# One row-maximum instruction and one eviction instruction for both heads of a softmax step

## The reference, cut to what matters

```python
# forgetting attention, 8 heads of 64, blocks of 128 queries, causal
logits = einsum('bhqd,bhkd->bhqk', qh, kh) + F_t - F_s        # masked above the diagonal
p = softmax(logits, axis=-1);  out = einsum('bhqk,bhkd->bhqd', p, v)
# cross attention, 4 heads of 256, 256 keys, no mask
p = softmax(q @ k.T / sqrt(256));  o = p @ v
# GQA, 8 query heads of 64 over 2 key heads, 512 keys, no mask
p = softmax(q @ k.T / 8);  o = p @ v
```

## Time and profile before

| | |
|---|---|
| median of 3 runs | 1402.72 us (1400.03 to 1402.81) |
| the profiled execution | 1399.9 us, its span 1398.1 us |
| granted TensorE clock, mean over the span | 0.994 |
| busy: PE, PEld, DVE, ACT, POOL | 1361.8, 1095.2, 660.2, 619.4, 613.9 us |
| `fox`: first scores to first product of the memory norm | 207.6 to 253.5 us |
| `xat`: first scores to the last product's start | 402.0 to 438.8 us |
| `gqa`: first scores to the first product of `out2` | 916.9 to 979.3 us |

### The profile page before, as it was taken

How to read it: one execution, slowest core, us unless ns; L and a number is a source line. 1 busy time by engine, 2 the same in 40 slices (tenths; PEclk the granted TensorE clock), 3 DMA queues, 4 the chain that set the end, 5 groups by cost and what they waited for, 6 DMA issues and landing times.

```text
span 1398.1 us, 17303 instructions
## 1 busy us (share of the span) xinstructions
PE 1361.8 (97%) x6544; PEld 1095.2 (78%) x6544; DVE 660.2 (47%) x973; ACT 619.4 (44%) x861; POOL 613.9 (44%) x448
## 2 busy tenths in 40 slices
PE   9999999999989999999999999988999999999999
PEld 7877955788876888888888887854878888888887
DVE  5434938355433444344343316588255555554111
ACT  5555228553444443434442123587245545554111
POOL 3444320374430456555564543411325555556453
PEclk9999999999999999999999999999999999999999
DMA  7222212142220244344436433200312222323422
GB/s 267 91 90 94 87 41 81 61 173 99 91 90 1 91 144 141 135 159 141 150 135 260 177 135 105 91 31 30 121 61 90 90 90 92 118 90 135 175 96 90
DMA packets 29055, 155.23 MB, mean 111 GB/s; under 512 B 3024, under 2 KB 4176, under 8 KB 14800
## 3 DMA queue, kind: packets, MB, share of 16 engines
q1 hardware_dynamic: 29008, 154.57, 31.5%
HBM read 152.46 MB, written 2.10 MB: 111 GB/s over the span
## 4 chain that ended last, share of the span: by engine, by line
issue 39%; PE 30%; POOL 26%; DVE 4%; DMA 0%; POOLq 0%; ACT 0%; SPq 0%
POOL wlo L388 26%; PE lin L1368 10%; PE lin L1370 10%; PE lin L1369 10%; DVE small L1026 1%; DVE expd L1037 1%; DMA raw<-w_slabs 0%; PE lin L1571 0%; DVE xl L906 0%; DVE win L1245 0%; DVE small L1030 0%; POOLq L397 0%; DVE wlo L914 0%; PE att L1433 0%; PE att L1439 0%
## 5 line engine op out<-in xcount | busy, mean ns | idle before, releaser
L388 POOL TENSOR_TENSOR wlo<-raw,whi 128x512 fp32r<-128x512 f32 x444 | 613.7, 1413 | 768.8 <-ACT whi L415 508.2
L1368 PE MATMUL lin<-xh,whi 128*128 128x512 f32 x1072 | 420.6, 392 | 4.0 <-POOL wlo L388 3.5
L1370 PE MATMUL lin<-xh,wlo 128*128 128x512 f32 x1072 | 417.6, 390 | 0.0
L1369 PE MATMUL lin<-xl,whi 128*128 128x512 f32 x1072 | 417.4, 389 | 0.0
L415 ACT ACTIVATE whi<-raw 128x2048 fp32r<-128x2048 f32 x66 | 126.6, 1918 | 266.7 <-PE lin L1370 260.4
L1368 PEld LDWEIGHTS lin<-xh,whi 128*128 128x128 f32 x1072 | 201.3, 188 | 52.5 <-issue 5.9
L1370 PEld LDWEIGHTS lin<-xh,wlo 128*128 128x128 f32 x1072 | 201.3, 188 | 42.1
L1369 PEld LDWEIGHTS lin<-xl,whi 128*128 128x128 f32 x1072 | 201.3, 188 | 41.4 <-issue 0.5
L1368 PE MATMUL lin<-fh,whi 128*128 128x512 f32 x352 | 137.1, 390 | 0.0
L1370 PE MATMUL lin<-fh,wlo 128*128 128x512 f32 x352 | 137.0, 389 | 0.0
L1369 PE MATMUL lin<-fl,whi 128*128 128x512 f32 x352 | 137.0, 389 | 0.0
(11 more groups left out here) (320 smaller groups left out, 1925.5 us busy)
## 6 DMA issues: line engine op xcount, KB each, us to landing
raw<-w_slabs SPq DMA_DIRECT2D x111, 1024.0 KB, 4.8
adar<-ada SPq DMA_DIRECT2D x48, 512.0 KB, 5.5
h<-x_t SPq DMA_DIRECT2D x4, 512.0 KB, 6.4
decay<-decay SPq DMA_DIRECT2D x4, 512.0 KB, 7.9
out_t<-h SPq DMA_DIRECT2D x3, 512.0 KB, 8.2
raw<-w_slabs SPq DMA_DIRECT2D x4, 256.0 KB, 7.0
rope<-rope SPq DMA_DIRECT2D x2, 512.0 KB, 7.3
memx<-mem_t SPq DMA_DIRECT2D x1, 1024.0 KB, 5.9
```

The source lines that it names most:

```text
L388: return nc.gpsimd.tensor_tensor(wlo[s][:, ks, :], raw[s][:, ks, :], f(whi[s][:, ks, :]), ALU.subtract)
L1368: nc.tensor.matmul(out, whi_, xhi_, start=first, stop=False)
L1369: nc.tensor.matmul(out, whi_, xlo_, start=False, stop=False)
L1370: return nc.tensor.matmul(out, wlo_, xhi_, start=False, stop=last)
```

## The change

The two row maxima of a step become one instruction, and so do the two evictions. For the maxima the two banks of a step must be one tensor, so `att` and `lin` are now halves of pair tensors (`att_pair`, `lin_pair`), at the same PSUM addresses. For the evictions the outputs of both heads must be one tensor, so `probt` became one tensor of both heads (`probs`), and its second buffer in `gqa` now lies in one piece over `tmp` and the start of the region, where its two halves lay before with the heads the other way round.

The waits follow: the maximum waits until both heads' scores are there, the eviction until both heads' transposes are there, and it raises `pt` by two at its end.

```diff
-        probt = [rg_sb(f"probt{i}", [P, TT, T], 64 + 8 * i) for i in range(2)]
+        probs = rg_sb("probs", [P, 2, TT, T], 64)
+        probt = [probs[:, i] for i in range(2)]
...
-        probt2 = [probt, [rg_sb("probt20", [P, TT, T], 0), sb("probt21", [P, TT, T], offset=tmp_at)]]
-        lin = [ctx.enter_context(nc.psum_tensor(f"lin{i}", [P, T], F32)) for i in range(4)]
-        att = [ctx.enter_context(nc.psum_tensor(f"att{i}", [P, T], F32)) for i in range(2)]
-        c_act = ctx.enter_context(nc.psum_tensor("c_act", [P, 2 * T], F32))
-        att += [c_act[:, T * i:T * (i + 1)] for i in range(2)]
+        probs2 = [probs, sb("probs2", [P, 2, TT, T], offset=tmp_at)]
+        probt2 = [[p[:, i] for i in range(2)] for p in probs2]
+        lin_pair = [ctx.enter_context(nc.psum_tensor(f"lin_pair{i}", [P, 2 * T], F32)) for i in range(2)]
+        att_pair = [ctx.enter_context(nc.psum_tensor(f"att_pair{i}", [P, 2 * T], F32)) for i in range(2)]
+        lin = [lin_pair[i // 2][:, T * (i % 2):T * (i % 2 + 1)] for i in range(4)]
+        att = [att_pair[i // 2][:, T * (i % 2):T * (i % 2 + 1)] for i in range(4)]
+        c_act = att_pair[1]
...
                     if j >= 2:
-                        for n in (2 * (j - 2), 2 * (j - 2) + 1):
-                            act.wait_ge(a["tp"], n + 1)
-                            nb = blocks(j - 2)
-                            nc.scalar.activation(out(n), tbank[n % 2][:, 0:P * nb].rearrange("p (s n) -> p s n", s=nb),
-                                                 ACT.Copy).then_inc(a["pt"], 1)
+                        act.wait_ge(a["tp"], 2 * (j - 2) + 2)
+                        made = tbank[:, :].rearrange("p (e s n) -> p e s n", e=2, n=P)[:, :, 0:blocks(j - 2), :]
+                        nc.scalar.activation(out(j - 2), made, ACT.Copy).then_inc(a["pt"], 2)
...
-                        for e in range(2):
-                            n = 2 * j + e
-                            dve.wait_ge(a["scores"], n + 1)
-                            last = nc.vector.tensor_reduce(ring(j, "max")[:, e:e + 1], att[n % 4][:, 0:width(j)], AX.X,
-                                                           ALU.max, negate=True)
+                        dve.wait_ge(a["scores"], 2 * j + 2)
+                        rows = att_pair[j % 2][:, :].rearrange("p (e n) -> p e n", e=2)[:, :, 0:width(j)]
+                        last = nc.vector.tensor_reduce(ring(j, "max"), rows, AX.X, ALU.max, negate=True)
```

More of the change, by code:

```diff
@@ L195, in build @@
         rope2 = rg_sb("rope2", [P, 2, T], 60)
[L197 to L203 removed]
+        assert tmp_at + 4 * TT * T == region
+        probs2 = [probs, sb("probs2", [P, 2, TT, T], offset=tmp_at)]
[5 more added lines that the diff above has]
+        c_act = att_pair[1]
         pool_banks = [lin[0:2], att[0:2]]
@@ L606, in beside_fox_act @@
                                              ).then_inc(n["hi"], 1)
-            softmax_act(fox, 16, 4, lin[0:2], lambda j: P * (j % 4 + 1), lambda j: j % 4 + 1, False,
-                        lambda n: probt[n % 2][:, 0:n // 2 % 4 + 1, P * (n // 2 % 4):P * (n // 2 % 4 + 1)], fox_hi, beside_fox_act)
+            softmax_act(fox, 16, 4, lin_pair[0], lambda j: P * (j % 4 + 1), lambda j: j % 4 + 1, False,
+                        lambda j: probs[:, :, 0:j % 4 + 1, P * (j % 4):P * (j % 4 + 1)], fox_hi, beside_fox_act)
             def group_norm(u):
@@ L706, in xat_hi @@
                     nc.scalar.activation(xah[:, 2 * hd + j, :], lin[2 + j][:, :], ACT.Copy).then_inc(xat["hi"], 1)
-            softmax_act(xat, 8, 2, lin[0:2], lambda j: M, lambda j: 2, True,
-                        lambda n: probt[0][:, 2 * (n // 4 % 2):2 * (n // 4 % 2) + 2, P * (n % 4):P * (n % 4 + 1)], xat_hi)
+            softmax_act(xat, 8, 2, lin_pair[0], lambda j: M, lambda j: 2, True,
+                        lambda j: probs[:, 0, 2 * (j // 2 % 2):2 * (j // 2 % 2) + 2, 2 * P * (j % 2):2 * P * (j % 2 + 1)
+                                        ].rearrange("p s (e n) -> p e s n", e=2), xat_hi)
             def activate_c(times):
@@ L813, in gqa_hi @@
                 nc.scalar.activation(xh[:, c, :], lin[c % 2][:, :], ACT.Copy).then_inc(gqa["hi"], 1)
-            softmax_act(gqa, 16, 4, lin[2:4], lambda j: T, lambda j: TT, True,
-                        lambda n: probt2[n // 8 % 2][n % 2][:, :, P * (n // 2 % 4):P * (n // 2 % 4 + 1)], gqa_hi,
+            softmax_act(gqa, 16, 4, lin_pair[1], lambda j: T, lambda j: TT, True,
+                        lambda j: probs2[j // 4 % 2][:, :, :, P * (j % 4):P * (j % 4 + 1)], gqa_hi,
                         beside_gqa_act, late=2)
```

## The result

| | before | changed |
|---|---|---|
| median | 1401.43 us (1399.44 to 1402.81, 8 runs) | 1405.14 us (1401.14 to 1406.14, 8 runs) |
| ratio | | 1.0031, interval [1.0018, 1.0044] |
| profiled execution | 1399.9 us, span 1398.1 | 1403.67 us, span 1401.9 |
| mean granted clock of the profiled execution | 0.994 | 0.994 |

The forecast was a difference of -0.1 us and a time of 1402.6 us. The time lies inside the stated range; the difference does not fit the forecast: the changed kernel is 3.7 us slower by the medians (3.4 by the means), and the whole interval lies above 1.

The account below looks back on a forecast made before the run. TensorE, 97% busy, was taken as the bound, with VectorE and ScalarE mattering only where it waits. `gqa` -0.55, `fox` +0.3, `xat` +0.15 made -0.1 us, so 1402.6 us from the runs' median; range 1399.5 to 1406.6.

Parts of the forecast that it names:

- The maxima: Merged reduction of 1024 columns takes 1.22 us against 1.29 for the pair; 14 steps of `gqa` gain 1.0 us.
- The evictions: Merged eviction takes 1.05 us against 1.08 to 1.11; gains taken as 0.3 us in `fox`, 0.15 in `xat`.
- covered delay in the middle of `gqa`: Evictions there start later, but 0.3 us of delay hide behind the wait for the bias product, 0.1 us to spare.
- The plain delays of the ends: Last steps of each stage: lost overlap delays `fox` by 0.6 us, `xat` by 0.3, `gqa` by 0.45.
- The steady gain: Gains in the steps, ahead of the stage ends: 1.0 us in `gqa`, 0.3 in `fox`, 0.15 in `xat`.
- The sum of the ends: Loss at the three stage ends, where nothing covers the lost overlap: 0.6 + 0.3 + 0.45 = 1.35 us.
- savings on the path: Rival, all stages: 40 maxima (2.8 us) and 40 evictions (2.0) all count, 4.8 us faster, 1397.9 us; chance 0.08.
- the lower bound: Lower end of the time range, stated as 1399.5: a gain of 0.3 with runs like the fastest shown, 1400.03.
- the merge that does not come about: Rival: merged instruction runs as two or slower, 0.08 us above the pair in 14 steps, 1404.8 us; chance 0.05.
- late evictions pace the stages: Rival, steps of all stages: unhidden transpose waits carried through ScalarE's order; 1410.6 us at full, 1406.6 at half; chance 0.20.
- The clash in `gqa` shifts: Rival: GpSimd's subtraction beside the norms near 951 us meets differently, about 2 us either way, 1400.7 or 1404.7; chance 0.12.

Follow-up runs that it names:

- the fillers: Changed kernel plus useless products in TensorE's waits at stage ends: 512 columns 1402.3 us, 1.0015; 128 columns 1400.18 us, 0.9995.
- `e3_split_ends`: Changed kernel with evictions per head again in the last two steps of each stage, merged elsewhere: 1398.72 us, ratio 0.9990 [0.9978, 1.0001].
- `e5_again`: The changed kernel unaltered, measured once more on another chip beside the kernel before: 1404.08 us, ratio 1.0019 [1.0007, 1.0031].

## Why the prediction was wrong

By its own steps:

- *The maxima*: right in cost, 1.22 us for 1024 columns and no cost for the second group. The 16 exponentials of `gqa` start within 49.47 us where they took 50.32: -0.85 against -1.0, and every profile with merged maxima stands at 49.5 to 49.6, every one without at 50.3.
- *The evictions*: 1.02 to 1.05 us, right. The pair took 1.08, so 0.03 to 0.06 us are won. The fixed part of 186 ns less the overlap of about 93 ns that the Trainium skill gives ("ScalarE: Activation LUTs", "What ACT_TABLE_LOAD costs") would have won 0.09 us; here the overlap is about 0.14 us (twice 0.610 less 1.08), and the measurement decides. The covered delay in the middle of `gqa` was indeed covered. In `fox` the forecast 0.3 us of gain did not come: first to sixteenth exponential 38.36 us against 38.12, +0.24. With the maxima alone merged it is 38.23 and with the evictions alone 38.28; what costs there is not shown.
- *The plain delays of the ends*: right in size. 0.68 us of idle time in `fox`, 0.42 in `gqa`'s tail (last exponentials to the next product, 9.91 against 9.49), against 0.6 and 0.45. For `xat` 0.3 was said; its waits grew by 0.50 in the trace, its tail by 0.4 where the clock is full, and the fit gives 0.3 +-0.2.
- *The steady gain*: forecast -1.45 (1.0 + 0.3 + 0.15). The fit's constant, -1.8 +-0.4, looks like it, and that is luck: -0.85 in `gqa` and +0.24 in `fox` leave about 0.6 us of gain in the traces, and the rest of the constant goes with 4 us less of lost clock (no run of `e3_split_ends` is at 0.991 or less, 6 of 35 of before on the same chip are).
- *The sum of the ends*: this step failed. "Here nothing covers the lost overlap", 1.35 us, was taken as delay alone. Measured are 4.8 us (3.2 + 0.9 + 0.6, rounded), 2.6 in `fox` above its forecast, while the plain delays in the traces are about 1.5. What was missing is the clock: behind the longer waits TensorE goes on at 1.2 GHz, and the same products take up to twice as long. At the end of `xat` the profiles show that directly; for `fox` the lost clock of the runs and the fillers show it, not the single profiles.

With the measured terms in place of the forecast ones, -1.8 + 4.8 = +3.0 us. Without the clock the terms of the traces make about +0.9 (-0.85 + 0.24 + 1.5), not -0.1; the other two to three microseconds are clock. The profile of before had the material. The ends show waits of 0.47 to 1.10 us, and TensorE stood at 0.50 after it had been starved; I used the latter for a rival about `gqa` alone. And the three times at hand fall in two groups, 1400.03 and 1402.72 to 1402.81; those are levels of the clock, which the forecast read as spread. Over eight runs the median before is 1401.43, so the base of 1402.72 was itself 1.3 us high, and that the 1402.6 lies only 2.5 us below the measured 1405.14 owes something to it.

Three prices are off by 0.1 to 0.2 us and change nothing: savings on the path make 1402.6 - 4.8 = 1397.8, the lower bound 1400.03 - 0.3 = 1399.7, and the 1404.8 of the merge that does not come about holds a lost gain of 1.0 us that is not named.

Of the rivals, *late evictions pace the stages* had the right sign, but not the mechanism: the 34 evictions in the steps cost nothing that can be measured. *The clash in `gqa` shifts* came nearest in kind. A slow stretch there at 955 to 959 is in before's profile, and not in the first of the changed kernel; its presence changed no period of the steps: 3.95, 5.67 and 3.05 us in `e5_again` with the stretch, 3.94, 5.67 and 3.05 in the first profile of the same kernel without. VectorE is busy for 1.93 of 2 us there.

## What to carry to other kernels

Merge two instructions of a helper engine where they run behind one another anyway, and keep them apart in the last steps of a stage, where the first head's eviction overlaps the second's transposes: one instruction is 0.03 to 0.07 us shorter than the two, and the lost overlap costs 0.45. Price every microsecond that TensorE waits at the end of a stage at more than itself, by a factor of two to five at the end of `fox` here, if waits of that kind already stand there. And look at the times of the single runs beside their mean granted clock before trusting one profile: a change can move runs between the levels, beside moving the levels themselves.

## What the hardware showed unexpectedly

- Runs of one kernel stand at levels tied to the mean granted clock: before at about 1397.3 us (0.996), 1399.8 (0.993 to 0.995) and 1402.8 (0.991); the changed kernel at 1399.2 to 1401.5 (0.995, 0.996) and 1403.6 to 1406.1 (0.994 and, most of them, 0.991 down to 0.989).
- A slow stretch costs nothing where another engine paces: at 955 us in `gqa` as told above, which may be part of why 1 us of lost clock costs 0.55.
- Waits longer by 0.2 to 0.3 us at the end of `xat`, 1.32 and 0.75 us instead of 1.10 and 0.47, go with a clock of 0.50 behind them: the product takes 5.25 to 5.40 us in all eight profiles that have these waits, 3.70 in the twelve that don't.
- Small products with no use (128 columns, 0.27 us each) into a free bank go with a full clock through waits of a microsecond, at the end of `fox` in all three profiles that have them and in the one with large ones; two of 512 columns take 1.88 us and are too long for such a wait.
